# Layer 0 of a two-layer encoder step on one core: other load order, gMLP value half inside its slabs, dt chain and spatial matmuls between slabs, inner-norm operands per tile

## What is computed

```python
h = rmsnorm(x, norm_mix[0])
u, v, z, xbc, dt_raw = split(h @ l0_w_in)        # 1024, 1024, 1024, 1536, 16 columns
# gMLP, 8 groups of 128 channels, chunks of 128 tokens
v = rmsnorm(gelu(v) per group) * gm_v_gain
ya = gelu(u) * (einsum('gij,bcjgd->bcigd', masked w_s, v) + b_s)
# Mamba-2 SSD, 16 heads
xbc, conv_state = causal_dwconv(xbc, width 4);  x, B, C = split(silu(xbc))
dt = softplus(dt_raw + dt_bias);  y, ssm_state = ssd_scan(x, dt, -exp(a_log), B, C)
yb = rmsnorm((y + d * x) * silu(z), ssm_norm)
x = x + concat(ya, yb) @ l0_w_out
```

## Time and profile before

| what | value |
|---|---|
| runs | 1999.78 us median (1998.51 to 2000.27) |
| profiled execution: span from the first to the last instruction | 1997.0 us |
| its own time | not given apart; the span stands 2.8 us under the median |
| PE busy / DVE / ACT / POOL | 94% / 48% / 31% / 44% of the span |
| mean granted PE clock | 0.955 |
| slabs (L310), three products | 900.0 + 890.5 + 883.3 us busy |
| one eviction, L1278 | 0.69 us mean, and about 0.2 for the 32 sample columns |
| read from HBM | 149.23 MB, 78 GB/s over the span |

### The profile page before, as it was taken

How to read it: one execution, slowest core, us unless ns; L and a number is a source line. 1 busy time by engine, 2 the same in 40 slices (tenths; PEclk the granted TensorE clock), 3 DMA queues, 4 the chain that set the end, 5 groups by cost and what they waited for, 6 DMA issues and landing times.

```text
span 1997.0 us, 34512 instructions
## 1 busy us (share of the span) xinstructions
PE 1869.7 (94%) x14129; PEld 1802.0 (90%) x14129; DVE 951.5 (48%) x1509; ACT 614.9 (31%) x886; POOL 877.9 (44%) x428
## 2 busy tenths in 40 slices
PE   3996997999999999999989999999989999999996
PEld 2995895789899999999989999999879999999995
DVE  1214585654755255155664444154445534524555
ACT  3241122223432222223443333233323422322342
POOL 4433142323754455456653333333335444544562
PEclk7995696999999999999999999999989999999998
DMA  4230020112123422222322222222212222222221
GB/s 141 85 105 26 23 85 9 43 43 74 64 85 109 135 85 95 96 77 71 106 75 82 82 71 72 94 75 83 72 42 80 93 87 85 95 96 82 71 92 45
DMA packets 49106, 156.23 MB, mean 78 GB/s; under 512 B 5969, under 2 KB 9937, under 8 KB 49010
## 3 DMA queue, kind: packets, MB, share of 16 engines
q1 hardware_dynamic: 43920, 146.75, 22.5%
q10 hardware_dynamic: 5090, 8.13, 1.2%
HBM read 149.23 MB, written 5.63 MB: 78 GB/s over the span
## 4 chain that ended last, share of the span: by engine, by line
PE 83%; DVE 9%; issue 3%; POOL 2%; ACT 2%; DMA 0%; DVEq 0%; SPq 0%; POOLq 0%; ACTq 0%
PE proj L310 73%; PE Q L891 8%; DVE arena L1361 1%; DVE op_lo L380 1%; DVE arena L1582 1%; ACT arena L601 1%; POOL ssq L396 1%; POOL arena L526 1%; DVE arena L1278 1%; PE Q L1111 0%; ACT op_hi L367 0%; DVE rstd L360 0%; POOL w_lo L405 0%; DVE x L1584 0%; DVE arena L1470 0%
## 5 line engine op out<-in xcount | busy, mean ns | idle before, releaser
L405 POOL TENSOR_TENSOR w_lo<-w_raw,w_hi 128x1024 fp32r<-128x1024 f32 (+2 forms) x276 | 654.8, 2373 | 817.3 <-ACT w_hi L331 817.0
L310 PE MATMUL proj<-op_hi,w_hi 128*128 128x256 f32 x4288 | 900.0, 291 | 43.6 <-POOL w_lo L405 20.6
L310 PE MATMUL proj<-op_hi,w_lo 128*128 128x256 f32 x4288 | 890.5, 289 | 0.0
L310 PE MATMUL proj<-op_lo,w_hi 128*128 128x256 f32 x4288 | 883.3, 287 | 0.0
L310 PEld LDWEIGHTS proj<-op_hi,w_hi 128*128 128x128 f32 x4288 | 689.2, 189 | 56.4 <-POOL w_lo L405 20.6
L310 PEld LDWEIGHTS proj<-op_lo,w_hi 128*128 128x128 f32 x4288 | 692.5, 189 | 0.0
L310 PEld LDWEIGHTS proj<-op_hi,w_lo 128*128 128x128 f32 x4288 | 688.0, 189 | 0.0
L331 ACT ACTIVATE w_hi<-w_raw 128x1024 fp32r<-128x1024 f32 (+2 forms) x276 | 284.7, 1032 | 710.1 <-PE proj L310 710.0
L1278 DVE TENSOR_TENSOR arena<-proj,rstd 128x512 f32<-128x512 f32 x153 | 105.6, 690 | 273.6 <-PE proj L310 273.0
L1285 DVE TENSOR_TENSOR x<-proj,x 128x512 f32<-128x512 f32 x72 | 49.8, 691 | 261.4 <-PE proj L310 261.4
L891 PE MATMUL Q<-arena 128*128 128x256 f32 (+9 forms) x604 | 140.4, 374 | 23.8 <-POOL arena L526 17.7
(11 more groups left out here) (149 smaller groups left out, 1003.0 us busy)
## 6 DMA issues: line engine op xcount, KB each, us to landing
w_raw<-in_w_gu SPq DMA_DIRECT2D x88, 512.0 KB, 3.3
w_raw<-in_w_down SPq DMA_DIRECT2D x32, 512.0 KB, 3.3
w_raw<-in_w_heads_a SPq DMA_DIRECT2D x30, 512.0 KB, 3.3
w_raw<-in_w_heads_b SPq DMA_DIRECT2D x18, 512.0 KB, 3.2
w_raw<-in_w_gate SPq DMA_DIRECT2D x16, 512.0 KB, 3.3
w_raw<-in_w_xbc SPq DMA_DIRECT2D x12, 512.0 KB, 3.4
w_raw<-in_w_down SPq DMA_DIRECT2D x16, 384.0 KB, 3.0
w_raw<-in_w_v SPq DMA_DIRECT2D x8, 512.0 KB, 4.9
```

The lines of the kernel that those rows point to most:

```text
L310: last = nc.tensor.matmul(proj[:, 2 * g.mod(2) + half, 0:size], w[:, lo:lo + P], o[:, at:at + size], start=(k == 0 and j == 0), stop=(k == ...
L405: nc.gpsimd.tensor_tensor(w_lo[:, c:c + width], w_raw[:, c:c + width], w_hi[:, c:c + width], ALU.subtract).then_inc(w_lo_done, 1)
```

## The change

The change rewrites the instruction lists of all five engines for layer 0.

- **Loads.** SP issues slab v0 first, then vec, the odd x tiles, slab v1, the constants, slabs v2 and v3. ACT issues the even x tiles, w_dt, gain_rows, w_spatial, the bias (now `bs_pad`, 128 rows with zeros below the first) and the ssm state, before its first split.
- **n_in.** ACT makes all eight `op_hi` first (with the split of slab 1 after the fourth), then the squares; DVE instead of POOL adds them. The mean square is taken after slab v1, and the wait for the constants stands there too.
- **v.** Each v tile is evicted to a ring of two, Gelu is applied, and PE turns it two slabs later; ACT copies and squares it, DVE sums it, all during the v slabs. `v_tok` is laid out by group (VT = 640 columns each). It and `u_g` now lie over the second operand buffer and the start of the arena.
- **dt.** The dt matmuls follow v7. Its turn comes after u1, DVE's bias after u1, the softplus after it has evicted u3, PE's time sums after slab u3 (waiting for `da_done`), and DVE's copies after u4.
- **spatial.** DVE scales groups 0 and 1 at u1, 2 to 4 at u2, 5 to 7 at u3 (`V_SCALED`), POOL applies the gain there. PE runs group g after slab u4+g, and the last four after xbc 0 to 3. The bias is one matmul of 512 columns and one of 32 for a group.
- **xbc.** Tap 0 is an ACT instruction (Identity with scale and bias).
- **SSD.** Slab outa 0 stands ahead of it; the other seven are placed 1, 2, 2, 1, 1 in the five chunks (`SSD_SLABS`).
- **z.** High, square, low and the sum of squares for `n_yb` are made for each tile inside the z loop, in op 1; the operand buffers of all later norms swap names.

The core of the diff:

```diff
+        U_FIRST = 4
+        V_SCALED = {1: (0, 1), 2: (2, 3, 4), 3: (5, 6, 7)}
+        SSD_SLABS = ((1, None), (2, 3), (4, 5), (6, None), (7, None))
...
+            first(0)
             sp.dma_start(vec[:, :], A["vec"]).then_inc(sem("vec_in"), 16)
-            for k in range(KD):
+            for k in range(1, KD, 2):
                 sp.dma_start(x[:, k * T:(k + 1) * T], A["x"][:, k * T:(k + 1) * T]).then_inc(sem(f"x_in{k}"), 16)
-            sp.dma_start(w_dt[:, :], A["w_dt"]).then_inc(sem("wdt_in"), 16)
-            weights("v")
+            first(1)
...
+            first(2)
+            first(3)
+            weights("v", RING)
             weights("u")
...
+            pool_squares(pool, "n_in", None)
+            for n in range(RING):
+                split_low(pool, At(n))
...
+            for n in range(KD):
+                low_ahead(pool, PH["u"], At(n))
+                for g in V_SCALED.get(n, ()):
+                    gain(g)
             phase("xbc")
+            low_ahead(pool, PH["outa"], At(0))
...
             pool_squares(pool, "n_yb", "n_in")
-            for n in range(KD):
-                pool_square(pool, "n_yb", At(n))
+            phase("z", lambda n: pool_square(pool, "n_yb", n))
...
+            for k in range(0, KD, 2):
+                act.dma_start(x[:, k * T:(k + 1) * T], A["x"][:, k * T:(k + 1) * T]).then_inc(sem(f"x_in{k}"), 16)
...
+            split_high(act, At(0))
             act.wait_ge(sem("vec_in"), 16)
-            split_high(act, At(0))
             for k in range(KD):
                 act.wait_ge(sem(f"x_in{k}"), 16)
-                act_operand(act, "n_in", At(k), part(x, k, 0, T))
...
+                run(part(op_hi[0], k, 0, T), part(x, k, 0, T), ACT.Copy, scale=col("mix0", k)).then_inc(nsem("hi"), 1)
+                if k == 3:
                     split_high(act, At(1))
+            for k in range(KD):
+                act_square(act, "n_in", At(k), part(x, k, 0, T))
...
+            for n in range(KD):
+                slab(pe, PH["v"], At(n), 0, (nsem("lo"), ncount("n_in", "lo", 1)) if n == 0 else None)
+                if n == 1:
+                    pe.wait_ge(consts_in, 16 * N_CONSTS)
+                    mean_square(pe, "n_in")
+                if n >= 2:
+                    v_turn(n - 2)
+            v_turn(KD - 2)
...
+            def spatial(g):
+
+                pe.wait_ge(sem("gm_vn"), g + 1)
+                if g >= 2:
+                    pe.wait_ge(sem("gm_ya"), 2 * g - 2)
+                q = 2 * (g % 2)
+                bias = bs_pad[:, g * P:(g + 1) * P]
+                mm(four(Q[:, q, :]), ones[:, :], bias.unsqueeze(1).broadcast_to([P, NC, P]), stop=False)
+                for c in range(NC):
+                    at = g * VT + c * P
+                    mm(Q[:, q, c * CH:(c + 1) * CH], v_tok[:, at:at + P], w_spatial[:, g * P:(g + 1) * P], start=False,
+                       stop=(c == NC - 1))
+                mm(Q[:, q + 1, 0:TS], ones[:, :], bias[:, 0:TS], stop=False)
+                mm(Q[:, q + 1, 0:TS], v_tok[0:TS, g * VT + TP:(g + 1) * VT], w_spatial[0:TS, g * P:g * P + TS],
+                   start=False).then_inc(sem("gm_s"), 1)
+
+            for n in range(KD):
+                slab(pe, PH["u"], At(n), 0)
+                if n == 0:
+                    v_turn(KD - 1)
...
+                elif n == 3:
+                    pe.wait_ge(sem("da_done"), 1)
+                    mm(Q[:, 1, 0:NP_], tri[:, :], da)
...
+                if n == U_FIRST:
+                    pe.wait_ge(sem("gm_mask"), 1)
+                    pe.wait_ge(sem("cs_copied"), 1)
+                if n >= U_FIRST:
+                    spatial(n - U_FIRST)
+            for n in range(XBC):
+                slab(pe, PH["xbc"], At(n), 0)
+                if KD - U_FIRST + n < GROUPS:
+                    spatial(KD - U_FIRST + n)
+            slab(pe, PH["outa"], At(0), 1, (sem("gm_lo"), 1))
...
+            for n in range(KD):
+                scaled(group("u", n), lambda c, w: part(u_g, n, c, w))
...
+                elif n == 1:
+                    dt_bias()
+                    dve.wait_ge(sem("gm_root"), 1)
...
+                elif n == 3:
+                    dt_softplus()
+                    nc.vector.memset(s_prompt, 0.0).then_inc(sem("s_zero"), 1)
+                elif n == 4:
+                    dt_sums()
+                for g in V_SCALED.get(n, ()):
+                    v_scale(g)
+                if n >= U_FIRST:
+                    ya_out(n - U_FIRST)
+                if n == U_FIRST + 1:
+                    dve.wait_ge(sem("gm_v_out"), 16)
...
                 dve.wait_ge(sem("z_silu"), (n + 1).v)
                 tt(part(xbc, n, 0, T), part(xbc, n, 0, T), zb, mul).then_inc(sem("yb_made"), 1)
+                dve_operand(dve, "n_yb", n, part(xbc, n, 0, T))
             each(dve, KD, z_body)
-            for n in range(KD):
-                dve_operand(dve, "n_yb", At(n), part(xbc, n, 0, T))
```

More of the change, by code:

```diff
@@ L667, in _ @@
-            act.wait_ge(sem("gm_sum"), NC + 1)
-            n_ = NC * GROUPS
-            run(ms_v[:, 0:n_], ms_v[:, 0:n_], ACT.Sqrt, bias=eps[:, 0:1], scale=1.0 / P)
-            run(ms_v[0:TS, n_:], ms_v[0:TS, n_:], ACT.Sqrt, "gm_root", bias=eps[0:TS, 0:1], scale=1.0 / P)
-            split_ahead(act, PH["xbc"], At(0))
-            split_ahead(act, PH["xbc"], At(1))
-            act.wait_ge(sem("gm_vn"), NC + 1)
-            act.dma_start(O["gm_v"], v_tok[0:TS, NC * D:(NC + 1) * D]).then_inc(sem("gm_v_out"), 16)
@@ L681, in conv_out, with conv_first @@
+            def conv_first(n):
+                q = n % 2
+                at = q * (T + 6)
+                act.wait_ge(sem("x_steps"), n * 5 + 2)
+                act.wait_ge(tile_read, PH["xbc"].g0 + n + 1)
+                run(conv[:, q * (T + 3):(q + 1) * (T + 3)], xpad[:, at:at + T + 3], ACT.Identity, "x_tap",
+                    bias=col("ssm_b", n), scale=col("ssm_w", n))
             def conv_out(n):
[L682 to L683 removed]
+                q = n % 2
+                act.wait_ge(sem("x_steps"), n * 5 + 5)
@@ L690, in conv_out, with chunk @@
                 run(part(xbc, n, TP, TS), conv[:, at + TP + 3:at + T + 3], ACT.Silu, "x_silu")
[L692 to L709 removed]
+            late = KD - U_FIRST
+            for n in range(XBC):
+                split_ahead(act, PH["xbc"], At(n))
+                conv_first(n)
+                if n <= GROUPS - late:
+                    ya_high(late - 1 + n)
+                if n:
+                    conv_out(n - 1)
+            conv_out(XBC - 1)
+            split_ahead(act, PH["outa"], At(0))
+            def chunk(p, rows):
                 c = NC if p == 0 else p - 1
@@ L729, in chunk @@
                     run(m, m, ACT.Exp, "decayed")
-                    if slabs and b % 2:
-                        split_ahead(act, PH["outa"], At(2 * p - 2 + b // 2))
+                    if b % 2 and SSD_SLABS[p][b // 2] is not None:
+                        split_ahead(act, PH["outa"], At(SSD_SLABS[p][b // 2]))
                 for half in range(2):
@@ L1021, in chunk @@
                     rows_of_cs(b)
-                if slabs:
-                    slab(pe, PH["outa"], At(2 * p - 2), 1, (sem("gm_lo"), 1))
+                first, second = SSD_SLABS[p]
+                slab(pe, PH["outa"], At(first), 1)
                 diagonal(0)
                 diagonal(1)
-                if slabs:
-                    slab(pe, PH["outa"], At(2 * p - 1), 1)
+                if second is not None:
+                    slab(pe, PH["outa"], At(second), 1)
                 diagonal(2)
@@ L1405, in _ @@
+                dve.wait_ge(tile_read, (group("xbc", n) + 1).v)
+                for tap in range(1, 4):
+                    dve.wait_ge(sem("x_steps"), n * 5 + 1 + tap)
+                    stt(out=acc, in0=xpad[:, at + tap:at + tap + T + 3], scalar=col("ssm_w", n + tap * XBC), in1=acc,
+                        op0=mul, op1=add).then_inc(sem("x_steps"), 1)
+                if late + n <= GROUPS:
+                    ya_low(late + n - 1)
+            add_to_x(group("outa", 0), At(0))
             dve.wait_ge(sem("decays"), 1)
@@ L1406, in _, with chunk @@
             dve.wait_ge(sem("s_in_loaded"), 16)
-            def chunk(p, rows, slabs):
+            def chunk(p, rows):
                 c = NC if p == 0 else p - 1
@@ L1444, in chunk @@
                 mixed(1)
-                if slabs:
-                    n = At(2 * p - 2)
-                    add_to_x(group("outa", n), n)
+                add_to_x(group("outa", first), At(first))
                 segments(2)
@@ L1451, in chunk @@
                 mixed(3)
-                if slabs:
-                    n = At(2 * p - 1)
-                    add_to_x(group("outa", n), n)
+                if second is not None:
+                    add_to_x(group("outa", second), At(second))
                 dve.wait_ge(sem("y_mm"), 4 * p + 4)
```

479 lines of the change are left out of this document (231 added, 248 removed).

## The result

The changed kernel takes 1934.20 us (median of 4 runs, 1933.46 to 1935.35), the kernel before, on the same chip, 2000.03 (4 runs, 1998.51 to 2000.45). The ratio is 0.9675, with a 95% interval of 0.9663 to 0.9686. The forecast was 1918 with a range to 1934: the direction was right, 16 us of the 82 did not come, and the time lies just above the range's upper end. In spans it is 17.2 us (1932.3 for 1915.1): the forecast adds 2.8 us for what lies between a span and a time, and in the profiled run of the changed kernel that is 1.8 (1934.12 against 1932.3).

A forecast was written before the change was run, and what follows sets the result against it. PE bounds the kernel, its dense slabs leaving nothing to gain; layer 0's waits and lower clock do. Gains of 18.5 at the start and 63.4 up to outb 1 take span 1997.0 to 1915.1, time 1918, range 1903 to 1934.

The forecast's parts named there:

- Part 1, the start: Load and split order up to slab v2: PE starts near 11.5, v2 at 37 for 55.6, gain 18.5 us.
- Part 2, v and u: v, u slabs and turns 90.2 us, including 2 for lower clock; dt slab 6.0; waits 11.5 behind u3, 2.0 at u4.
- The step behind u3: PE's wait for the dt chain after slab u3, not hidden by a slab: 11.5 us, ends 7.3 and 14.
- Part 3: Spatial matmuls at full clock: 2.3 us a group, eight 18.4 in place of 51.89 and waits of 17.7 and 3.0.
- Part 4: xbc to SSD: 12 dense xbc slabs 72.2 us, slab outa 0 6.0, remaining wait 1.8, SSD 127.5.
- SSD: 20.5 + 2 x 28.6 + 2 x 24.9 = 127.5: SSD's sample chunk at full clock, two two-slab and two one-slab chunks, a one-slab chunk saving 3.7 us; ends 125 and 136.
- rival (b): Lower clock in SSD's sample and one-slab chunks, spatial matmuls keeping much old price: +8, up to +19, 1926 to 1940; chance 0.17.
- Part 5: z and outb: operands made inside z slabs, z stays 47.9 us; what follows takes 8.6 in place of 20.1.
- The sum: All terms from slab v2 to slab outb 1: 396.3 us for 459.7 before, gain 63.4, with the start 81.9.
- (a): Rival: dt chain not slowed (7.3 us), v2 at 32, spatial 2.0 a group: 12 us less, 1906; chance 0.14.
- (c): Rival: PE stays below 2.4 GHz after pauses behind v1 and u3, slower than before, up to 2050; chance 0.01.
- (d): Rival: x or slab 1 arrives late behind 2 MB of ACT's loads, start gains nothing: 1937; chance 0.07.

The follow-up runs named there:

- e12: Changed kernel with the dt chain's first DVE instruction in a two-input form instead of a one-input form: 1934.59 us in one run.
- e4: Changed kernel with value groups 2 to 4 scaled at u3 after the dt chain and 5 to 7 at u4: 1928.48 us.
- e5: Changed kernel with time sums behind u4, first spatial group behind u5, groups 2 to 7 scaled at u4 and u5: 1920.43 us.
- e1: Changed kernel with idle matmuls in PE's SSD waits, 20 in the sample chunk and 24 in each one-slab chunk: 1926.79 us.
- e2: Changed kernel with outa slabs placed as before the change, none ahead of SSD or in the sample chunk, two in each other: 1926.84 us.
- e6: Changed kernel with ACT's four large loads issued after its fourth split: 1932.37 us.
- e7: Changed kernel with outa slab 0 ahead of SSD, the others 0, 2, 2, 2, 1, and 24 idle matmuls in the last chunk: 1926.65 us.

## Why the prediction was right or wrong

**What bounds the kernel**, and where the change could gain: right. All 64.8 us came ahead of outb 1.

**Part 1, the start**: v2 at 35.6 for 37 forecast, gain 20.0 for 18.5. Slab 1 at 14.50 for 15; the path was slab 1, hi 4, lo 4 and then the rest of two slabs, as written. The first four steps ran at 1.36 us each, the lower level, as written too, although the granted clock reads 1.00 there (16 matmuls in 3.70 us of the row from 11 to 15; at the full level it is 10 or 11 in 1 us). From 18.63 on the pitch was that of the full level, and slab 1 was done at 27.7 for 30. The pause for the norm's root was 6.8 for 7. The rate of 0.28 MB a us was a mean with the first 2 us in it: in the windows of the kernel before, its one queue moved 322 GB/s from 3 to 4 us and 401 from 11 to 12, with the 16 DMA engines full.

**Part 2, v and u**: slab v2 lost 2.7 for 2. The step behind u3 was the one that is not behind a slab, as written, and cost 14.0 for 11.5, its upper end. The trace of before showed one DVE operation held by one POOL instruction; with several queued on POOL, DVE was held until the last of them (5.32 us, and 5.37 in e12), and with the gains moved away only once for each split (e4, e5). The Trainium skill (SBUF — State Buffer, "Who interferes with whom") has the lock between the two engines, and the trace agrees that it is one; that an operation waits for four instructions in a row is this case's measurement. The second wait was 1.5 for 2.0, slab u4 lost 2.5 for 2.

**Part 3**: right. 2.23 to 2.47 us a group for 2.3 (the terms written out add up to 2.4); the slabs between them 6.19 in place of 6.02, 1.4 in all.

**Part 4**: xbc dense as forecast, the wait ahead of SSD 0.8 for 1.8. **Then the step that failed: "SSD: 20.5 + 2 x 28.6 + 2 x 24.9 = 127.5".** It was 143.3 us. From x turns to x turns the chunks took 29.1, 29.95, 28.6, 28.5 and 27.2: the sample chunk is 8.6 over its term, the chunk behind it 1.4, the two with one slab 5.9 together. The working of a one-slab chunk gave PE's extra wait rightly (2.4 us for 2.2), and then took all else, y's matmuls too, from rows at the full clock. A two-slab chunk has PE busy through y; with a slab less there is a pause of 2.4 us right ahead of it, the granted clock fell to 0.50, and the 20 matmuls took 7.07 in place of 3.52. The slab saved 6.0, and 2.4 and 3.55 of it went back: nothing is left of it. In the sample chunk, the larger part, "at full clock" failed: DVE's first product takes 2.41 us beside POOL's split (1.23 in a prompt chunk, with the same 1024 columns), PE waits 2.4 us, and the slab takes 8.74; behind it PE waits 2.7 us more, and the 24 matmuls take 9.17. The clock then stays low for 14 us in all, into the next chunk, for which 28.6 was a price at the full level; the kernel before had that loss too (135.8 us of SSD from 311.48 to 447.24, for 134.2 by these prices). e1 shows that it is the clock: of the one-slab chunks it gave all of the y matmuls' 3.55 us back, of the sample chunk 5.2 of the 8.6 us. Why that chunk takes 23.9 with the clock kept is not shown. e2 shows that the placing lost 7.4 us as a whole. This was rival (b), 1926 to 1940, in its SSD half, at twice the 8 us that it had put on it (15.8; its two terms, 8 and 19, give 1926 to 1937, or 1945 together). It had "for it" that the clock was seen low there, and it was given 0.17: the windows were read for where the clock was low, not for what pause comes ahead of each fall.

**Part 5**: 8.2 for 8.6. **The sum** from v2 to outb 1 was 414.9 for 396.3: of the 18.6, SSD has 15.8, the dt wait 2.5. The other terms cancel to within 1 us. From outb 1 to the end it is 1481.8 us for 1481.7, so the fetches of unrolled loops cost nothing that the span shows.

**Rivals**: (a) fell with the u3 wait; (c) did not come, since PE was back at 1.0 within one slab wherever a slab stood behind the pause (5.5 us into v2, 5.0 into u4), but behind the sample chunk's second pause, with small matmuls only, it took 14 us; of (d) 2.3 us was true (e6).

## What to carry to other kernels

A slab removed from between two dependent steps is worth its time only if PE is busy without it: price what stands behind the new pause at the lower clock too, and look in the trace for the shortest pause that is followed by a fall. Compare such stages in more than one run: the pause of 2.4 us was followed by 6.8 us of the lower clock or by 3.4, and the short ones by none or by 3.4. A small chain on DVE should be placed where POOL has nothing queued, and its consumer further than it seems to need: with POOL's gains moved away the wait went from 14.0 to 8.8, with the consumer one slab later as well to 5.0, with two to none. Together with e6's loads and a placing that leaves the sample chunk without a slab this gave 1905 us. Idle matmuls keep the clock only where they fit into the pause; where they stand in the way they cost the same again.

## What was not expected of the hardware

- A DVE operation of 80 columns, by itself 0.19 us, was held 5.3 us over four whole and one begun POOL instructions, in either form (e12); it got in only when POOL had nothing more to run. A reciprocal of the same columns wasn't held by a split (0.65 us in e4).
- Single pauses of PE's of 2.4 to 2.7 us were followed by 3.4 us (e5), 6.8 us, or 14 us (behind the sample chunk's slab) at a granted clock of 0.50, that is 1.2 GHz; the first two are of the same chunks with the same instructions. The pauses of 1.11, 0.74 and 0.53 us that follow each other at the end of every two-slab chunk were mostly not, but once in e1 and once in e7 they were, for 3.4 us each.
- Two queues with x and weights moved 413 GB/s from 11 to 15 us with the 16 DMA engines full; the one queue of the kernel before had filled them too (401 GB/s from 11 to 12 us). A transfer of 512 KB still took 10.4 us from its issue to its landing, beside all the others, and 2.3 less with four of them moved away (e6).
- The first slabs' clock came back at two different times with the same work, 1.5 us apart at slab v2.
